# Second feed-forward block of a two-part network: eight half-token fp32 products against seven

## The reference

```python
D_MODEL, SEQ, DEPTH, D_FF = 1024, 256, 2, 2816

def swiglu(h, w_gate, w_up, w_down):
    return (jax.nn.silu(h @ w_gate) * (h @ w_up)) @ w_down

for l in range(DEPTH):                      # first_block
    ...                                     # mixer: x = x + gate1 * mix
    h = modulate(rms_norm(x, norm2_g[l]), shift2, scale2)
    x = x + gate2[:, None, :] * swiglu(h, ffn_w_gate[l], ffn_w_up[l], ffn_w_down[l])
# second_block starts with rms_norm_2(x, pre_norm[0]) and a projection by a_w_in
```

## Time and profile before

| | us |
|---|---|
| profiled execution, its own time | 1144.42 |
| its span, first to last instruction | 1142.6 |
| TensorE busy, of the span | 1077.2 (94%) |
| VectorE / ScalarE busy | 467.6 (41%) / 290.3 (25%) |
| feed-forward stage of `l = 1`, from its third hidden chunk to the last down product | 525.34 to 739.52 |
| mean granted clock of TensorE | 0.991 |

### The profile page before, as it was taken

How to read it: one execution, slowest core, us unless ns; L and a number is a source line. 1 busy time by engine, 2 the same in 40 slices (tenths; PEclk the granted TensorE clock), 3 DMA queues, 4 the chain that set the end, 5 groups by cost and what they waited for, 6 DMA issues and landing times.

```text
span 1142.6 us, 19466 instructions
## 1 busy us (share of the span) xinstructions
PE 1077.2 (94%) x8485; PEld 902.1 (79%) x8485; DVE 467.6 (41%) x928; ACT 290.3 (25%) x695; POOL 64.0 (6%) x84
## 2 busy tenths in 40 slices
PE   6879999999999999899999999999996899999997
PEld 4648888888888857588888888878886688888686
DVE  8996445444314728622000000234914561602632
ACT  6512500000002564512000000124413251202632
POOL 3010011110101000000000000000003100000000
PEclk9999999999999999999999999999999999999999
DMA  9995889899844443263535432444440003544220
GB/s 292 350 317 172 282 322 376 323 350 358 317 161 119 139 143 108 81 200 111 194 115 171 160 113 77 143 142 133 128 162 6 5 3 111 184 150 145 75 75 37
DMA packets 120271, 195.67 MB, mean 171 GB/s; under 512 B 4161, under 2 KB 103115, under 8 KB 113787
## 3 DMA queue, kind: packets, MB, share of 16 engines
q1 hardware_dynamic: 109754, 131.15, 35.8%
q0 software_dynamic: 10144, 62.92, 14.5%
q10 hardware_dynamic: 288, 0.36, 0.1%
HBM read 191.53 MB, written 1.05 MB: 169 GB/s over the span
## 4 chain that ended last, share of the span: by engine, by line
PE 81%; DVE 11%; ACT 3%; issue 3%; DMA 1%; SPq 0%; DVEq 0%; ACTq 0%
PE psum L665 59%; PE psum L1027 13%; DVE arena L1766 4%; PE psum L940 2%; PE psum L1551 1%; ACT arena L2629 1%; DVE sq L1766 1%; DVE arena L1772 1%; DVE arena L1936 1%; PE psum L1526 1%; DVE arena L2030 1%; ACT sq L2629 1%; DVE arena L1769 1%; DVE xT L1772 1%; PE psum L1675 1%
## 5 line engine op out<-in xcount | busy, mean ns | idle before, releaser
L665 PE MATMUL psum<-hT,ring 128*128 128x256 f32 x1392 | 311.4, 382 | 2.9 <-DVE hT L1772 2.0
L665 PEld LDWEIGHTS psum<-hT,ring 128*128 128x128 f32 x1392 | 263.3, 191 | 42.3 <-issue 7.2
L2629 ACT ACTIVATE arena<-psum 128x512 f32<-128x512 f32 (+6 forms) x225 | 101.5, 479 | 615.9 <-PE psum L665 568.8
L665 PE MATMUL psum<-hT,arena 128*128 128x256 f32 (+2 forms) x984 | 165.0, 339 | 4.6 <-DVE hT L1766 4.6
L665 PEld LDWEIGHTS psum<-hT,arena 128*128 128x128 f32 (+2 forms) x984 | 143.5, 181 | 24.5 <-issue 6.4
L1766 DVE TENSOR_TENSOR arena<-arena,psum 128x256 f32<-128x256 f32 (+2 forms) x76 | 39.0, 530 | 264.9 <-ACT arena L2629 235.5
L665 PE MATMUL psum<-arena 64*64 64x64 f32 (+6 forms) x2252 | 87.9, 240 | 18.7 <-issue 14.0
L665 PEld LDWEIGHTS psum<-arena 64*64 64x64 f32 (+3 forms) x2252 | 68.6, 140 | 32.2 <-issue 28.3
L1027 PE MATMUL psum<-arena,ring 128*128 128x256 f32 x384 | 85.1, 380 | 0.0
L1027 PEld LDWEIGHTS psum<-arena,ring 128*128 128x128 f32 x384 | 72.6, 190 | 11.0 <-issue 1.2
L665 PE MATMUL psum<-ring,arena 128*128 128x256 f32 (+2 forms) x288 | 73.3, 415 | 0.5 <-ACT arena L2629 0.5
(11 more groups left out here) (281 smaller groups left out, 1043.8 us busy)
## 6 DMA issues: line engine op xcount, KB each, us to landing
aring<-in_ada_w POOLq DMA_DIRECT2D x36, 1024.0 KB, 8.4
ring<-in_a_w_in SPq DMA_DIRECT2D x14, 1024.0 KB, 5.4
arena<-in_ffn_w_gate SPq DMA_DIRECT2D x12, 1024.0 KB, 7.5
arena<-in_ffn_w_up SPq DMA_DIRECT2D x12, 1024.0 KB, 7.9
ring<-in_ffn_w_down SPq DMA_DIRECT2D x12, 1024.0 KB, 5.1
ring<-in_ffn_w_gate SPq DMA_DIRECT2D x10, 1024.0 KB, 9.9
ring<-in_ffn_w_up SPq DMA_DIRECT2D x10, 1024.0 KB, 7.1
arena<-in_ffn_w_down SPq DMA_DIRECT2D x10, 1024.0 KB, 5.0
```

What stands on the lines that cost most here:

```text
L665: return eng.matmul(dst, w, x, start=first, stop=last)
L2629: return eng.activation(dst, x, f, **k)
```

## The change

The products of `l = 1`, apart from the first two hidden chunks, are made by Strassen's scheme in its form with seven products. The input is cut in two halves of its channels and two of its tokens (128 each), the weight in halves of its rows, and the other side of the weight is the pair gate and up (for the down product: two chunks of output). Sums of token blocks (`t1..t4`) and of weight blocks (`s1, s2, s4`, and one in place of a panel's part) are made by VectorE from SBUF. TensorE makes seven products with 128 tokens moving in place of eight (four with 256). VectorE and ScalarE put the results together out of PSUM.

The down product no longer runs beside gate and up: it follows them, output pair by output pair (`i`), over three panels `q` of eight rows of chunks (the last of six) by 256 columns.

```diff
+                for j in range(1, NDN):                         # TensorE, gate and up
+                    ...
+                    eng.wait_ge(*next_bank(p1, pool))
+                    multiply(p1, g[:, lo], hT3[:, lo, 0:P]).then_inc(*pe.signals("half_products"))
+                    eng.wait_ge(done("weights_combined"), 4 * n + 2)
+                    if j == 1:
+                        eng.wait_ge(done("tokens_combined"), 28 * HALVED.index(l) + 3)
+                    multiply(p6, s2, t2).then_inc(*fills(p6))
+                    eng.wait_ge(done("weights_combined"), 4 * n + 3)
+                    multiply(p7, u[:, lo], t3).then_inc(*pe.signals("half_products"))
+                    multiply(p5, s1, t1).then_inc(*pe.signals("half_products"))
+                    eng.wait_ge(done("first_copied"), copy_of(l, j))
+                    multiply(p1, g[:, hi], hT3[:, hi, 0:P], False).then_inc(*fills(p1))
+                    eng.wait_ge(done("weights_combined"), 4 * n + 4)
+                    eng.wait_ge(done("halves_read"), 2 * nth + 2)
+                    multiply(p5, s4, hT3[:, hi, P:T], False).then_inc(*fills(p5))
+                    eng.wait_ge(done("halves_read"), 2 * nth + 1)
+                    multiply(p7, u[:, hi], t4, False).then_inc(*fills(p7))
+                for i in range(KC // 2):                        # TensorE, down
+                    for q in range(DOWN_PANELS):
+                        ...
+                        multiply(px, 0, w[:, :, 0, 0:P], hp[:, :, 0, 0:P])
+                        eng.wait_ge(done("weights_combined"), 4 * down_unit(l, d) + 4)
+                        multiply(px, 1, s2, t2)
+                        multiply(px, 2, w[:, :, 0, P:2 * P], hp[:, :, 0, P:T])
+                        last = multiply(px, 3, s1, t1)
+                        multiply(py, 0, w[:, :, 1, 0:P], hp[:, :, 1, 0:P])
+                        multiply(py, 1, s4, hp[:, :, 1, P:T])
+                        last = multiply(py, 2, w[:, :, 1, P:2 * P], t4)
 ...
+            def combine_weights(l, j, part):                    # VectorE
+                if part == 1:
+                    tt(s1, u[:, lo], u[:, hi], ALU.add).then_inc(*v.signals("weights_combined"))
+                elif part == 2:
+                    tt(s2, s1, g[:, lo], ALU.subtract).then_inc(*v.signals("weights_combined"))
+                elif part == 3:
+                    tt(u[:, lo], g[:, lo], u[:, lo], ALU.subtract).then_inc(*v.signals("weights_combined"))
+                else:
+                    tt(s4, g[:, hi], s2, ALU.subtract).then_inc(*v.signals("weights_combined"))
 ...
+                for j in range(1, NDN):                         # VectorE, one step
+                    if j < NDN - 1:
+                        combine_weights(l, j + 1, 2)
+                    tt(u2, ps(p6), u2, ALU.add).then_inc(*v.empties(p6))
+                    if j < NDN - 1:
+                        combine_weights(l, j + 1, 3)
+                    else:
+                        combine_down(l, 0)
+                    tt(u3, ps(p7), u2, ALU.add).then_inc(*v.signals("halves_read"))
+                    tt(up[:, :, half_1], ps(p5), u3, ALU.add).then_inc(*v.signals("halves_read"))
+                    if j < NDN - 1:
+                        combine_weights(l, j + 1, 4)
+                    else:
+                        combine_down(l, 1)
+                    if j % 2 == 0:
+                        combine_hidden(l, [j - 2, j - 1])
+                    tt(hid[:, two, half_1], ps(p5), u2, ALU.add).then_inc(*v.empties(p5))
+                    if j < NDN - 2:
+                        combine_weights(l, j + 2, 1)
+                    tt(up[:, :, half_0], ps(p7), u2, ALU.add).then_inc(*v.empties(p7))
+                    tt(hid[:, two, :], hid[:, two, :], up, ALU.mult).then_inc(*v.step())
+                combine_down(l, 2)
+                combine_down(l, 3)
+                ahead = 4
+                for i in range(KC // 2):
+                    for d in range(ahead, min(3 * i + 6, DOWN_PANELS * KC // 2)):
+                        combine_down(l, d)                      # four sums of 512 or 384 columns
+                    ahead = 3 * i + 6
+                    down_outputs(i)                             # seven adds of 128, then xT3 += gate * out
+            def begin_recurrent(i):                             # at the end of down_outputs(i)
+                ts(raw_a[:, c, :], xT3[:, c, :], cols("pre_norm_2", 0, KC)[:, c:c + 1], None, ALU.mult)
+                if i > 1:
+                    sum_squares("squares", 12, (i - 1,))
 ...
+                for j in range(1, NDN):                         # ScalarE, one step
+                    act(first_sum[j % 2], ps, ACT.Copy).then_inc(*s.signals("first_copied"))
+                    act(hid[:, two, 0:P], ps, ACT.Silu).then_inc(*s.empties(p1))
+                    act(hid[:, two, P:T], hid[:, two, P:T], ACT.Silu).then_inc(*s.signals("silu_ready"))
```

More of the change, by code:

```diff
@@ L430, in blocks_kernel @@
         a9 = stat[:, 0:2 * T].rearrange("p (m t) -> p m t", t=T)
+        halves = Carver(m1.o + KC)
+        sums = halves(4 * 3 * HALF // 2)
+        h_sums = halves(KC * T).rearrange("p (x k t) -> p x k t", x=4, t=P)
+        first_sum, third_sum = [[halves(T).rearrange("p (m t) -> p m t", t=P) for _ in range(2)] for _ in range(2)]
+        up_rows = [halves(2 * T).rearrange("p (m t) -> p m t", t=T) for _ in range(2)]
         latent = [m1(2 * T).rearrange("p (k t) -> p k t", t=T) for _ in range(2)]
@@ L1040, in swiglu @@
                     if j == 0:
[L1041 to L1056, removed]
+                        first_chunks(l, h_base, g, u)
+                    for m in range(2) if j else ():
                         c = 2 * j + m
-                        if c == 0:
-                            continue
                         eng.wait_ge(*next_bank(("gu", l, c)))
@@ new lines, in _, with combine_hidden @@
+            hid_done = [None]
+            def combine_hidden(l, js):
+                h = hid_pair(js)
+                b11, b12, b21, b22 = [h[:, :, r, t:t + P] for r in range(2) for t in (0, P)]
+                t1, t2, t4 = [hid_sum(x, js) for x in range(3)]
+                eng.wait_ge(*hid_done[0])
+                tt(t1, b12, b11, ALU.subtract).then_inc(*v.signals("tokens_combined"))
+                one = v.last
+                tt(b12, b22, b12, ALU.subtract).then_inc(*v.signals("tokens_combined"))
+                eng.wait_ge(*one)
+                tt(t2, b22, t1, ALU.subtract).then_inc(*v.signals("tokens_combined"))
+                eng.wait_ge(*v.last)
+                tt(t4, b21, t2, ALU.subtract).then_inc(*v.signals("tokens_combined"))
@@ L2795, in _, with squares @@
                     .then_inc(*s.signals("squares"))
-            def squares(r):
+            def squares(r, ahead=lambda pair: None):
                 for pair in range(4):
+                    ahead(pair)
                     if r >= len(UPDATES):
@@ L2985, in _ @@
             shift(hT3, 1, 3, 3 * KC)
-            swiglu(1)
-            squares(3)
+            swiglu_of_halves(1)
+            squares(3, lambda pair: copy_down(1, pair))
             root(("ms", 4))
```

279 lines of the change are left out of this document (262 added, 17 removed).

## The result

The changed kernel takes 1123.36 us (median of four runs, 1121.39 to 1123.68); the kernel before took 1142.9 us on the same chip (four runs). The ratio is 0.982, with a 95% interval of 0.980 to 0.984: 20 us faster. The forecast was 1123.3 us, with a range of 1118 to 1130.

A forecast was written before the change was run, and what follows sets the result against it. TensorE, busy throughout the stage, was taken as the bound. Stream +193.6 - 214.2, first step +0.9 and end -0.4 sum to -20.1 us, so 1143.36 - 20.1 = 1123.3 us; 8-in-10 range 1118 to 1130.

The forecast's parts named there:

- The stream: TensorE's products in the stage: 1736 records at 111.5 ns, 193.6 us, in place of 214.2 us.
- the twenty single-column records: Profile row of the kernel before, where the load alone can set the pace: 2.23 us / 20 = 111.5 ns a record.
- The 108.5 ns of the transposes: Sixteen 128-column transposes in the earlier profile, taken as how near matmuls can stand; lower end of stream, 188.4 us.
- VectorE in a steady step: Gate and up steps: 8.5 us of VectorE work in 12.5 us, margin 1.1 us before `halves_read`, no TensorE wait.
- The first step: First step of gate and up: TensorE waits 0.9 us, once, for VectorE's sums and reads.
- The end: From the stage's end to the first record on hT: 0.4 us gained, bounds 0 and 1.
- Down product and panels: Down product's VectorE sums (11.8 us per 17.2 us output pair) and panel landings by DMA: nothing to pay.
- VectorE late in each step: Rival at the margin before `halves_read`: TensorE waits for VectorE, +5.7 us, time 1129 us; chance 0.13.
- the loads in series: Rival in the long stream: load and matmul follow each other, 220 ns a record, time 1311 us; chance 0.03.
- The matmul's own pace: Rival in the stream: matmul's 108.5 ns holds, not the load's; stream 188.4 us, time 1118 us; chance 0.08.
- the gain is given back elsewhere: Rival: panels in 1 KB pieces come late or the tail's chain is longer, 5 us, time 1128 us; chance 0.06.

The follow-up runs named there:

- the 64 tokens: Changed kernel with all 868 products of the stage moving only the first 64 of their 128 tokens: 1122.19 us, ratio 0.981 to the kernel before.
- the two wider forms: Changed kernel with gate and up products moving 160 columns (1149.38 us, ratio 1.0055), and the 256-token products of the kernel before (1142.9 us).
- the one with the later copies: Changed kernel with GpSimd's two copies of 1536 columns behind the stage waiting until hT is made: 1123.38 us in one execution.
- the first trace: Changed kernel with three more VectorE sums of 1024 columns ahead of the read of p7 in nine steps: 1137.28 us, ratio 0.994.

## Why the prediction was right

By its own steps:

- **The stream, +193.6 - 214.2.** Measured 193.85 and 214.11 us: -20.26 for -20.6. The price of a record was taken as 111.5 ns from the twenty single-column records and is 111.67. That it is not the matmul's pace is shown by the 64 tokens, and the records with narrower loads leave the load; that load and matmul overlap in a stream of 1736 records is shown by the stage itself. The 108.5 ns of the transposes, which the prediction took as the matmul's pace, come with shorter loads (141 ns), so that row could never have been the price here; as the matmul's pace it was near (109.2 by the two wider forms).
- **VectorE in a steady step.** The order of reads and sums came out as worked out, the margin as 1.1 us, as reckoned, or 1.0 up to the load that waits. VectorE's busy time was counted as 130 us and is 119.6, overlapping records counted once. The experiment with the one-column sums shows that nothing of it is on the path; the one with three more sums ahead of the read of p7 shows that a wait would have stood at `halves_read`.
- **The first step, +0.9.** Wrong: TensorE does not wait. I had added the recorded lengths of VectorE's operations, but independent ones that follow each other start closer than that: two begin at 528.63 and the next at 530.90, so 1.13 us each, though one is recorded with 1.22. VectorE in the first step, from the changed kernel's timeline:

```profile
528.63 2.35 DVE L1942 TENSOR_TENSOR arena<-arena 128x1024 f32<-128x1024 f32 x2
530.90 1.22 DVE L1942 TENSOR_TENSOR arena<-ring 128x1024 f32<-128x1024 f32 x1
532.04 0.41 DVE L1942 TENSOR_TENSOR arena<-arena,psum 128x256 f32<-128x256 f32 x1
532.37 1.22 DVE L1942 TENSOR_TENSOR arena<-arena,ring 128x1024 f32<-128x1024 f32 x1
533.50 0.42 DVE L1942 TENSOR_TENSOR arena<-psum,arena 128x256 f32<-128x256 f32 x1
533.84 1.22 DVE L1942 TENSOR_TENSOR ring<-ring 128x1024 f32<-128x1024 f32 x1
534.97 0.88 DVE L1942 TENSOR_TENSOR arena<-psum,arena 128x256 f32<-128x256 f32 x2
```

  Some 80 ns of an operation lie beside the next, unless that one needs its result (the two reads of 534.97 stand 0.45 us apart). The stage starts 1.9 us later than the sum assumed, and by it the read of p5 would end at 537.0; it ends at 535.85. Eleven such overlaps on the way make 0.9 of these 1.15 us. The rest of p5 starts at 536.23, its load at 536.12: 0.4 and 0.3 us to spare in place of 0.9 us missing. The experiment with three more sums ahead confirms how thin it is: 3.36 us of its 3.6 became a wait.
- **The end, -0.4.** Measured -1.2, beyond the bound of 1 us. The norm's product stands 4.8 us behind the stage's end in place of 5.2, as reckoned. The rest came from a place that I hadn't looked at, the first scaling of `hT`, 0.93 us for 1.66, because GpSimd's copy beside it ends earlier. The copy starts when a DMA has landed, 8.1 us behind the stage's end before and 6.9 here (6.5 to 7.1 in the seven experiments that leave it in place); no term of the prediction was about it. The end of the changed kernel, to be laid beside the earlier trace rows:

```profile
721.15 4.95 PE L743 MATMUL psum<-aring,ring 128*128 128x256 f32 x22
721.35 0.69 DVE L1942 TENSOR_TENSOR arena<-psum,arena 128x128 f32<-128x128 f32 x3 [0.69 <-PE psum L1183]
722.08 1.00 DVE L1948 SCALAR_TENSOR_TENSOR xT<-arena,ada,xT 128x256 f32<-128x256 f32 x2
723.46 1.47 DVE L1942 TENSOR_TENSOR stat<-stat,sq 128x512 f32<-128x512 f32 x2
724.96 0.42 DVE L1942 TENSOR_TENSOR stat<-stat 128x256 f32<-128x256 f32 x1
725.94 0.59 PE L743 MATMUL psum<-stat,const_sb 128*128 128x256 f32 x2
729.95 2.40 PE L743 MATMUL psum<-hT,ring 128*128 128x256 f32 x10 [1.26 <-DVE hT L1948]
```

- **Down product and panels, nothing.** No record of the down product comes late; the DMA share is 0.50 at 158 GB/s, where 0.49 and 158 were reckoned.

The sum was -20.1 us. With the measured terms it is -20.3 + 0 - 1.2 = -21.5 within stage and end. The profiled spans differ by 21.0, the medians of the same chip by 19.5; the rest are the 1.9 us ahead of the stage and the 1.4 behind it. The mechanism and the size of the large term were right. That the median came out within 0.1 us of the forecast is luck: two small terms were wrong by about 1 us each, both towards too little gain, and differences ahead of the stage and between executions, which no term was about, took that back. The row of 50 records in 12.72 us had shown the slow clock behind the stage, and the prediction passed over it.

The rivals: VectorE late in each step and the loads in series are out by the stage itself, which has no wait and no distance above 112 ns. The matmul's own pace (108.5 ns, 1118 us) is out by the stage and by the 64 tokens. That the gain is given back elsewhere is out: the stretches behind the stage are shorter, not longer.

Loads and matmuls of the whole array overlap here for 1736 records, at 111.67 ns where one behind the other would be about 220. The rule of the Trainium skill (TensorE: Matmul & The Clock Gate, section "Part 3: Packing small matmuls — row/col tiling"), that a load overlaps only when the row group differs, does not hold in these runs.

What stays open: when a wait makes the clock fall. It fell after waits of 3.1 and of 2.0 us and after none of 0.8 to 1.5 us at these places; but a wait of 1.95 us further on, near 847 us, was followed by a fall in the changed kernel and by none in the one with the later copies, so the length alone doesn't decide. Open too are the 1.9 us ahead of the stage: the one trace of the kernel before begins it at 525.4, the nine others at 526.6 to 528.4 us.

## What to carry to other kernels

Price a fp32 matmul with 128x128 weights as the greater of the load's pace and the matmul's, and read both from distances between starts, not from recorded lengths; a scheme that halves the columns pays down to the point where the load takes over, here about 131 columns, and gains less than its count of products says: 9.5% of the stage in place of 12.5. Of the 3 points that are missing, by the estimate of 109.2 ns, the matmul's fixed part takes 1 and the load 2. Work added to an engine with time to spare is free by its place, not by its amount: find the one read that the bound engine waits for, and put sums behind it. Before calling a tail's chain understood, look for what other engines do beside each of its links.

## What the runs showed of the hardware

- Loads of 128x128 fp32 weights pace at 111.67 ns in a stream of 1736 records, and at 111.63 with 64 columns in the matmul; with 160 columns a record takes 135.8 ns, with 256 it is 215.8. Transposes, whose loads are recorded with 141 ns in place of 192, start 109 ns apart.
- Independent operations on VectorE that follow each other start about 80 ns before the recorded end of the one before: 1.13 us apart for 1.22 us of length with 1024 columns, 0.34 for 0.42 with 256.
- A wait of TensorE of 3.1 us was followed, 0.7 us after work began again, by some 3.3 us at a granted clock of 0.50 (1.2 GHz), with 15 records at 213 ns (1.6 us lost); one of 2.0 us in the kernel before was followed by the same after 0.6 us (1.7 us lost). Eight waits of 0.8 us in the first trace were not.
- A scaling of 256 columns on VectorE takes 0.48 us alone; beside a copy of 1536 columns on GpSimd it ended 0.28 us after the copy's end in nine traces, 0.60 to 1.66 us long, while the copy kept its 1.46 us.
